# Gate and up products of a SwiGLU block: eight of eleven pairs by seven half-size products each, with weight sums made in memory

## The chip, the cores and the metric

The kernel runs on one core of a Trainium2 chip. The metric is the device time of one execution in microseconds, the median over runs. A core has TensorE (PE, with its weight loads as PEld), VectorE (DVE), ScalarE (ACT), GpSimd (POOL) and SyncE (SP, which here only issues DMAs). Each engine works through its own instructions in order and waits on semaphores for the others.

## What is computed

One encoder block over 512 tokens of width 1024, float32 in and out. Three gated branches are merged, and then comes the feed-forward part that the change touches:

```python
hf = _rms(x, g_ffn[l])
x = x + (jax.nn.silu(hf @ w_gate[l]) * (hf @ w_up[l])) @ w_down[l]     # D_FF = 2816
return _rms(x, g_final)
```

`w_gate` and `w_up` are 1024 x 2816, so each has 22 column tiles of 128, or 11 pairs of tiles.

## The kernel before

**Split products.** Every float32 operand is held as two fp32r tensors, a rounded high part and the rest, the low part. A product (`product`, L1652 to L1656) is three matmuls into one bank: high x high, low x high, high x low. So each weight tile of 128x1024 needs a load into `raw` (SP, `next_weights`), a rounding copy to `w_hi` (ACT, L619), and a subtraction `raw - w_hi` to `w_lo` (POOL, `low_weights`, L528). There are two slots of each (`NS`, `RAW` = 2). `w_rounded`, `w_ready` and `w_used` count the three steps and the tile's release by TensorE.

**Order of the stages.** The branches, then `w_out` (tiles `T_WO` to `T_FF`-1), then gate and up, then the down projection. Below, a "pair" is one of the 11 iterations of gate and up: four tiles (two gate, two up), each eight products of 128x512 in its bank, banks 0 to 3. TensorE's `feed` does them, in a loop from the second pair on.

**The normalisation.** The tokens' reciprocal root mean square isn't known when the first gate tile starts. `h_hi` and `h_lo` therefore hold x times the gain only, and VectorE multiplies each finished bank by `rstd` (`silu<-bank,rstd`, `parts<-bank,rstd`, `odd<-bank,rstd`).

**What follows a pair.** ACT applies SiLU to the gate half (L911); VectorE multiplies it with the up half, so that `parts[0:2]` and `odd` hold the hidden values of the pair: `a21, a11` and `a22, a12`, each a quarter of 128x256 (feature tile by token half). VectorE makes four sums of the quarters (`s_1` to `s_4`: L1037 twice, L1513, L1515). ACT's `split_hidden` rounds them into `ops` (128x1024, L916) and `op4` (128x256, L918), VectorE subtracts for their low parts (`ops<-parts,ops`, `op<-parts,op`), and `ff_lo` counts pairs done. SP stores `odd` to memory (`store_half`).

**The down projection** is already done by seven half-size products in place of eight. The sums of its weight blocks are made in memory: SP copies blocks of `w_down` to `mix_dram` (`copy_blocks`, two copies a pair, one behind each weight tile from tile `T_MIX` = 16 on), and POOL issues three accumulating DMAs a pair (`weight_sums`, one pair for every two weight tiles). Down weights are then loaded as units (`load_unit`, `round_unit`) and threes (`load_three`).

**Issue orders** are written out by hand for each engine; ACT's for a pair is: two SiLUs, three weight roundings, `split_hidden`, one weight rounding.

Of the kernel before, what the change touches and what calls it, by code (L numbers as in the profile page):

```python
# [16 lines left out]
P = 128  # L17
D = 1024
T = 512
M = 256  # L20
# [29 lines left out]
T_DN = T_FF + 4 * (KF // 2)  # L50
PAIRS = KF // 2
GROUPS = ((0, 2), (2, 5), (5, 8), (8, 11))
# [31 lines left out]
def build(nc, xt_d, xtok_d, mem_d, mtok_d, small_d, sgu_d, row_d, w_d, dn_d, mix_d, half_d, x1_d, out_d):  # L84
# [7 lines left out]
    with ExitStack() as ctx:  # L92
# [32 lines left out]
        h_lo = at("h_lo", o_h + 16384, [P, KD, T], R)  # L125

# [7 lines left out]
        x1_sq = [at(f"x1_sq{i}", o_a + ((6 + i) * PAIRS + 3) * 4 * HALF, [P, KD, KD, 32]) for i in range(2)]  # L134
# [9 lines left out]
        raw_d = at("raw_d", o_h + 12288, [P, TILE])  # L144
        raw_x = [at(f"raw_x{i}", o_x + 8192 + 4096 * i, [P, TILE]) for i in range(2)]
        raw_e = at("raw_e", o_e + 12288, [P, TILE])
        unit_raw = [raw[:, 0, :], raw[:, 1, :], raw_c[:, :], *(r[:, :] for r in raw_x), raw_d[:, :], raw_e[:, :]]
# [7 lines left out]
        unit_hi = [at("hi_x", o_x, [P, TILE], R)[:, :], w_hi[:, 0, :], w_hi[:, 1, :],  # L155
                   at("hi_c", o_h + 24576, [P, TILE], R)[:, :]]
        unit_lo = [at("lo_x", o_x + 4096, [P, TILE], R)[:, :], w_lo[:, 0, :], w_lo[:, 1, :],
# [43 lines left out]
        ops = at("ops", o_a, [P, 4, 2, PAIRS, HALF], R)  # L201
        op4 = at("op4", o_f, [P, 2, PAIRS, HALF], R)
        second = at("second", o_a + 2 * PAIRS * HALF * 4, [P, PAIRS, T])
        second_lo = at("second_lo", o_a + 2 * PAIRS * HALF * 4, [P, PAIRS, T], R)
        second_hi = at("second_hi", o_a, [P, PAIRS, T], R)
# [28 lines left out]
        rstd = at("rstd", o_d2 + 512, [P, T])  # L234
        o_d3 = o_d2 + 2560
# [21 lines left out]
        def sems(names):  # L257
            return [sem(n) for n in names.split()]

        raw_loaded = [sem(f"raw_loaded{i}") for i in range(RAW)]  # L260
# [10 lines left out]
        consts, wst_masked, hbias_ready, tables_ready = sems("consts wst_masked hbias_ready tables_ready")  # L271
# [5 lines left out]
        tok_sq, tok_std, diag_x, diag_m, wide_x, wide_m, rstd_ready, mrstd_ready = sems(  # L277
            "tok_sq tok_std diag_x diag_m wide_x wide_m rstd_ready mrstd_ready")
# [3 lines left out]
        var_ready, vstd_ready, vln_ready = sems("var_ready vstd_ready vln_ready")  # L282
# [8 lines left out]
        uc_ready, pow_ready, pads_ready, ca0_ready, ba_ready, ca_ready = sems(  # L291
            "uc_ready pow_ready pads_ready ca0_ready ba_ready ca_ready")
# [6 lines left out]
        mix_copied, mix_b12, mix_t2, mix_t4, half_stored = sems("mix_copied mix_b12 mix_t2 mix_t4 half_stored")  # L299
        unit_loaded = [sem(f"unit_loaded{i}") for i in range(7)]  # L300
        unit_half, unit_dve, p5_done, s1_ready, s5_ready = sems("unit_half unit_dve p5_done s1_ready s5_ready")
# [6 lines left out]
        row_loaded, out_dve, out_act, out_stored = sems("row_loaded out_dve out_act out_stored")  # L308
# [55 lines left out]

        block = ctx.enter_context(nc.Block())
# [3 lines left out]
        def _(sp):  # L369
# [11 lines left out]
            def next_weights(t):  # L381
                sp.wait_ge(w_ready, t + 1 - RAW)
                load_weights(t % RAW, t, w_d[t, :, :])
# [19 lines left out]
            def copy_blocks(i, j):  # L403

                if i:
                    sp.wait_ge(mix_copied, 32 * i)
                sp.dma_start(long_rows(mix_d[i, 2 * j:2 * j + 2]), long_rows(dn_d[2 * i + j]),
                             max_dma_last_dim=8 * TILE).then_inc(mix_copied, 16)

            for t in range(8, T_WO):  # L410
                next_weights(t)
                if 0 <= t - T_MIX < 2 * PAIRS:
                    copy_blocks(*divmod(t - T_MIX, 2))
                if t == T_J2 - 2:
                    sp.wait_ge(ba_ready, ROUNDS)
                    sp.wait_ge(ca_ready, ROUNDS)
                    for i in range(len(X_PARTS)):
                        load_x(i)
# [11 lines left out]
            def unit_split(eng, k):  # L430

                if k in UNIT_DVE:
                    eng.wait_ge(unit_dve, UNIT_DVE.index(k) + 1)
                else:
                    eng.wait_ge(w_ready, T_DN + UNIT_POOL.index(k) + 1)

            def load_unit(k):

                if k < 2:
                    sp.wait_ge(w_ready, T_DN - 1 + k)  # L440
                elif k == 5:
                    sp.wait_ge(w_used, T_DN)
# [5 lines left out]

            for t in range(T_WO, T_DN):
                next_weights(t)  # L450
                i, j = divmod(t - T_FF, 4)
# [4 lines left out]
                if i == 8 and j == 0:  # L456
                    sp.wait_ge(x1_moved, 16 * 8)
                    sp.wait_ge(mix_t4, 16 * PAIRS)
                    for k in (2, 3, 4):
                        load_unit(k)  # L460
# [19 lines left out]
            def load_half(g):  # L480
                k0, k1 = GROUPS[g]
                sp.dma_start(second[:, k0:k1, :], half_d[k0:k1, :, :].rearrange("k p n -> p k n")
                             ).then_inc(half_loaded[g], 16)

            for k in range(2):
                load_unit(k)
            load_unit(5)
# [3 lines left out]
            unit_split(sp, 4)  # L491
# [5 lines left out]
            sp.wait_ge(w_used, T_DN + 10)  # L497
# [8 lines left out]
            sp.wait_ge(w_used, T_DN + PAIRS)  # L506
            sp.dma_start(g_row[:, :], row_d).then_inc(row_loaded, 16)
# [13 lines left out]
        def _(pool):  # L521
# [25 lines left out]
            def two_rows(blocks):  # L547
# [1692 lines left out]
```

## Time and profile before

| | us |
|---|---|
| median of 3 runs | 772.1 (768.29 to 773.09) |
| profiled execution | 769.09 |
| its span, first to last instruction | 767.3 |
| outside the span | 1.8 |
| TensorE busy | 758.7 |
| VectorE busy | 490.0 |
| ScalarE busy | 354.9 |
| GpSimd busy | 343.2 |
| gate and up, from the first matmul to the last | 416.0 to 656.3 |

The span minus busy time is an engine's idle time. Matmuls are pipelined: a matmul's own duration in the profile (389 ns at 512 columns) is longer than the step from one to the next, so steps are what adds up. Gate and up take 240 of the 767 us.

### The profile page before, as it was taken

Reading aid. Unit: us, or ns where it says so; the run is one execution under the profiler, and the core shown is the slowest. Engines: PE = TensorE matmul, PEld = TensorE weight load, DVE = VectorE, ACT = ScalarE, POOL = GpSimd, SP = SyncE. Lnnn points to the kernel's source line nnn. Section 1 sums busy time; section 2 is a strip of 40 time slices with the busy share of each in tenths; the row PEclk is TensorE's granted clock in tenths of the full one; section 3 lists DMA queues with packets and bytes.
Section 4 is the critical chain, followed back from the end, with each engine's and each line's share of the span. In section 5 each row is a group of like instructions: output and inputs, shape, how many; then the busy total and the mean of one; then the engine's idle time right before and its main releaser. Section 6 shows DMA issues by size and latency. Waiting matters only on the chain.

```text
span 767.3 us, 9696 instructions
## 1 busy us (share of the span) xinstructions
PE 758.7 (99%) x3562; PEld 629.5 (82%) x3562; DVE 490.0 (64%) x708; ACT 354.9 (46%) x529; POOL 343.2 (45%) x202
## 2 busy tenths in 40 slices
PE   8999999999999999999999999999999999999997
PEld 7788887788888888888888888888888888888885
DVE  6999998684848484246767645455444455636686
ACT  6896567644545333634343423232323323435554
POOL 4456666356565543444444444444545455730000
PEclk9999999999999999999999999999999999999999
DMA  8743668199876752222233633333325333677853
GB/s 263 299 158 132 225 200 265 61 262 270 229 208 147 179 189 106 83 92 100 83 111 102 199 98 120 107 111 117 102 98 189 122 97 123 221 243 262 287 201 117
DMA packets 41491, 126.17 MB, mean 164 GB/s; under 512 B 4720, under 2 KB 6896, under 8 KB 38256
## 3 DMA queue, kind: packets, MB, share of 16 engines
q1 hardware_dynamic: 39376, 113.92, 42.9%
q0 software_dynamic: 1936, 11.54, 8.0%
q8 instruction: 21, 0.34, 0.2%
q10 hardware_dynamic: 144, 0.26, 0.1%
q14 instruction: 14, 0.11, 0.0%
HBM read 118.62 MB, written 30.15 MB: 194 GB/s over the span
## 4 chain that ended last, share of the span: by engine, by line
PE 91%; ACT 3%; DVE 3%; issue 1%; DMA 1%; SPq 0%; POOL 0%; ACTq 0%
PE bank L1654 24%; PE bank L1655 24%; PE bank L1656 24%; PE bank L2018 4%; PE bank L2019 4%; PE bank L2020 4%; ACT uc L679 1%; DVE s5p L1037 1%; PE bank L1895 1%; PE bank L1770 1%; PE bank L1787 1%; DMA xT<-xt_dram 1%; ACT w_hi L619 1%; DVE h_lo L1042 1%; PE bank L1869 0%
## 5 line engine op out<-in xcount | busy, mean ns | idle before, releaser
L528 POOL TENSOR_TENSOR w_lo<-raw,w_hi 128x1024 fp32r<-128x1024 f32 x90 | 221.5, 2461 | 273.8 <-ACT w_hi L619 273.8
L619 ACT ACTIVATE w_hi<-raw 128x1024 fp32r<-128x1024 f32 x112 | 118.7, 1060 | 311.4 <-PE bank L1656 306.8
L1654 PE MATMUL bank<-h_hi,w_hi 128*128 128x512 f32 x608 | 238.5, 392 | 0.2 <-POOL w_lo L533 0.2
L1656 PE MATMUL bank<-h_hi,w_lo 128*128 128x512 f32 x608 | 236.7, 389 | 0.0
L1655 PE MATMUL bank<-h_lo,w_hi 128*128 128x512 f32 x608 | 236.6, 389 | 0.0
L1654 PEld LDWEIGHTS bank<-h_hi,w_hi 128*128 128x128 f32 x608 | 114.2, 188 | 24.6 <-issue 1.0
L1655 PEld LDWEIGHTS bank<-h_lo,w_hi 128*128 128x128 f32 x608 | 114.2, 188 | 23.8 <-issue 0.5
L1656 PEld LDWEIGHTS bank<-h_hi,w_lo 128*128 128x128 f32 x608 | 114.1, 188 | 23.6
L533 POOL TENSOR_TENSOR w_lo<-raw,w_hi 128x512 fp32r<-128x512 f32 x48 | 67.1, 1417 | 50.3 <-ACT w_hi L619 43.2
L1037 DVE TENSOR_TENSOR lo<-raw,hi 128x1536 fp32r<-128x1536 f32 (+1 forms) x19 | 33.3, 1758 | 24.3 <-ACT hi L948 24.2
L1037 DVE TENSOR_TENSOR ops<-parts,ops 128x1024 f32 x11 | 25.9, 2352 | 27.8 <-ACT ops L916 24.6
L948 ACT ACTIVATE hi<-raw 128x1536 fp32r<-128x1536 f32 (+1 forms) x19 | 27.3, 1442 | 32.0 <-PE bank L2020 27.2
L1037 DVE TENSOR_TENSOR parts<-bank,rstd 128x512 f32<-128x512 f32 x11 | 7.6, 691 | 46.0 <-PE bank L1656 46.0
L1037 DVE TENSOR_TENSOR odd<-bank,rstd 128x512 f32<-128x512 f32 x11 | 7.6, 692 | 41.7 <-PE bank L1656 41.7
L1037 DVE TENSOR_TENSOR th<-bank,rstd 128x512 f32<-128x512 f32 x16 | 10.9, 682 | 30.7 <-PE bank L1656 30.6
L813 ACT ACTIVATE yaf<-bank 32x128 f32<-32x128 f32 x64 | 25.0, 390 | 4.5 <-PE bank L1870 3.8
L1037 DVE TENSOR_TENSOR parts<-odd,parts 128x256 f32<-128x256 f32 x11 | 26.4, 2398 | 0.4
L1654 PE MATMUL bank<-mg_hi,w_hi 128*128 128x512 f32 x64 | 25.0, 390 | 0.0
L1655 PE MATMUL bank<-mg_lo,w_hi 128*128 128x512 f32 x64 | 24.9, 389 | 0.0
L1656 PE MATMUL bank<-mg_hi,w_lo 128*128 128x512 f32 x64 | 24.9, 389 | 0.0
L1477 DVE SCALAR_TENSOR_TENSOR h_lo<-xT,small,h_hi 128x512 fp32r<-128x512 f32 x8 | 18.1, 2265 | 9.0 <-ACT h_hi L632 9.0
L679 ACT ACTIVATE uc<-uT 32x512 f32<-32x512 f32 x16 | 17.9, 1119 | 0.4
(331 smaller groups left out, 1411.4 us busy)
## 6 DMA issues: line engine op xcount, KB each, us to landing
raw<-w_dram SPq DMA_DIRECT2D x112, 512.0 KB, 3.3
mix_dram<-down_dram SPq DMA_DIRECT2D x22, 512.0 KB, 6.2
raw<-down_dram SPq DMA_DIRECT2D x26, 256.0 KB, 4.0
raw<-mix_dram SPq DMA_DIRECT2D x26, 256.0 KB, 3.7
mix_dram<-down_dram POOLq DMA_DIRECT2D x11, 512.0 KB, 9.6
mix_dram<-mix_dram POOLq DMA_DIRECT2D x22, 256.0 KB, 6.0
half_dram<-odd SPq DMA_DIRECT2D x11, 256.0 KB, 4.2
second<-half_dram SPq DMA_DIRECT2D x3, 768.0 KB, 6.5
```

Of the source, the lines that this page charges most:

```text
L528: nc.gpsimd.tensor_tensor(w_lo[:, s, :], raw[:, s, :], fv(w_hi[:, s, :]), ALU.subtract).then_inc(w_ready, 1)
L533: return nc.gpsimd.tensor_tensor(w_lo[:, s, c], raw[:, s, c], fv(w_hi[:, s, c]), ALU.subtract)
L619: nc.scalar.activation(w_hi[:, slot, :], raw[:, slot, :], ACT.Copy).then_inc(w_rounded, 1)
L679: nc.scalar.activation(dst[:, :, q, :], src[:, :, :, j], ACT.Copy).then_inc(uc_ready, 1)
L948: nc.scalar.activation(hi3[u % 2][:, 0:pieces(u), :], raw3[u % 3][:, 0:pieces(u), :], ACT.Copy).then_inc(rounded3, 1)
L1037: return V.tensor_tensor(out, a, b, op)
L1654: mm(out, a[0], b[0], start=first, stop=False)
L1655: mm(out, a[0], b[1], start=False, stop=False)
L1656: return mm(out, a[1], b[0], start=False, stop=last)
L2018: mm(bank[b][:, :], a[0], w[0], start=first, stop=False)
L2019: mm(bank[b][:, :], a[0], w[1], start=False, stop=False)
L2020: return mm(bank[b][:, :], a[1], w[0], start=False, stop=last)
```

## The change

The first three pairs (`PLAIN`) stay as they are. Each of the other eight (`TURNS`) becomes a turn: the 256 gate columns x 1024 rows are taken as a 2x2 grid of blocks (128 output features x 512 rows each), the normed tokens as a 2x2 grid (512 rows x 256 tokens), and the 2x2x2 block product is done by seven block products (`form_product`: 4 products of three 128x256 matmuls) instead of eight; the same for up. A turn has seven weight tiles (`FORMS`) of two blocks each, and 14 block products. What this takes:

- *Weight sums in memory:* 16 more jobs of copies and accumulating adds like those of the down projection, before these; the copies sit behind weight tiles 16 to 69 and the adds run to tile 78.
- *Operands:* the sums of token blocks (`t1` to `t4`) need tokens that are normed. VectorE multiplies x by gain and `rstd` (`norm_rows`), ACT rounds (`round_normed`), VectorE subtracts (`low_rows`), makes the sums (`forms_of_h`) and their low parts, all of it between the steps of the second and third pair. The plain pairs read copies in `hu_hi`, `hu_lo`.
- *Results:* the sums of products are made by VectorE from banks (15 `combine` a turn, 128x256); two products are first copied out of their banks by ACT (`copy_first`).
- *Weights:* a ring of three slots. Tiles 0, 2, 4, 6 of a turn get their low part from GpSimd, tiles 1, 3, 5 from VectorE (`low_weights`). Each tile is two DMAs of 256 KB.
- The loops of all engines are written out; semaphores are merged; `ops` is laid out by pair.

The core of the diff. Which engine finishes a tile, and GpSimd's share:

```diff
+        def low_done(eng, n):
+            i, j = divmod(n, FORMS)
+            if j % 2:
+                eng.wait_ge(w_ready_dve, 3 * i + j // 2 + 1)
+            else:
+                eng.wait_ge(w_ready, T_ST + 4 * i + j // 2 + 1)
...
+            for n in range(ST_TILES):
+                if n % FORMS % 2 == 0:
+                    pool.wait_ge(w_rounded, T_ST + n - 1)
+                    nc.gpsimd.tensor_tensor(ring_lo[n % 3], ring_raw[n % 3], fv(ring_hi[n % 3]), ALU.subtract
+                                            ).then_inc(w_ready, 1)
```

ScalarE, its new steps and its order in a turn:

```diff
+            def round_forms(n):
+                if n < 2:
+                    act.wait_ge(w_used, T_ST - 1 + n)
+                elif n > 2:
+                    act.wait_ge(product_done, 2 * (n - 2))
+                act.wait_ge(raw_loaded[n % 3], (0 if n % 3 == 2 else 16 * (T_ST // 2 - 1)) + 32 * (n // 3 + 1))
+                nc.scalar.activation(ring_hi[n % 3], ring_raw[n % 3], ACT.Copy).then_inc(w_rounded, 1)
+            def copy_first(turn, which):
+                act.wait_ge(product_done, 14 * turn + (1, 3)[which])
+                if which:
+                    act.wait_ge(ff_lo, PLAIN + turn + 1)
+                elif turn:
+                    act.wait_ge(combined, 15 * turn - 12)
+                out = (a_st[:, :], parts[:, 0, :])[which]
+                nc.scalar.activation(out, bank[4 - 4 * which][:, 0:HALF], ACT.Copy).then_inc(s_copied, 1)
...
+            for turn in range(TURNS):
+                n = FORMS * turn
+                round_forms(n + 2)
+                copy_first(turn, 0)
+                split_hidden(PLAIN + turn - 1)
+                round_forms(n + 3)
+                copy_first(turn, 1)
+                round_forms(n + 4)
+                round_forms(n + 5)
+                silu_forms(turn, 0)
+                round_forms(n + 6)
+                if turn + 1 < TURNS:
+                    round_forms(n + 7)
+                    round_forms(n + 8)
+                    silu_forms(turn, 1)
```

VectorE, in the second and third pair, and then in a turn:

```diff
+            scaled_gate(1, 0)
+            norm_rows(range(0, 4))
+            scaled_gate(1, 1)
+            norm_rows(range(4, 8))
+            scaled_up(1, 0)
+            low_rows(range(0, 5))
+            scaled_up(1, 1)
+            low_rows(range(5, 8))
+            hidden_sums(1)
+            low_hidden(1)
+            scaled_gate(2, 0)
+            forms_of_h()
+            scaled_gate(2, 1)
+            low_forms_a()
+            scaled_up(2, 0)
+            low_forms_b()
+            scaled_up(2, 1)
+            low_weights(1)
...
+            for turn in range(TURNS):
+                n, i = FORMS * turn, PLAIN + turn
+                hidden_sums(i - 1)
+                dve.wait_ge(s_copied, 2 * turn + 1)
+                combine(turn, 2, u2_st[0][:, :], gb, a_st[:, :], ALU.subtract)
+                low_weights(n + 3)
+                low_hidden(i - 1)
+                dve.wait_ge(s_copied, 2 * turn + 2)
+                combine(turn, 4, u2_st[1][:, :], ub, a21, ALU.subtract)
+                combine(turn, 5, g11, a_st[:, :], ga, ALU.add)
+                combine(turn, 6, g21, u2_st[0][:, :], gc, ALU.add)
+                low_weights(n + 5)
+                combine(turn, 7, u2_st[0][:, :], u2_st[0][:, :], gd, ALU.subtract)
+                dve.wait_ge(combined, 15 * turn + 5)
+                combine(turn, 7, g22, u2_st[0][:, :], gc, ALU.add)
...
+                if turn + 1 < TURNS:
+                    low_weights(n + 8)
+                dve.wait_ge(ff_silu, 2 * i + 1)
+                combine(turn, 12, a21, a21, g11, ALU.mult)
+                combine(turn, 13, a22, a22, uc_, ALU.add)
+                combine(turn, 14, a11, ud, u2_st[1][:, :], ALU.subtract)
+                dve.wait_ge(ff_silu, 2 * i + 2)
+                dve.wait_ge(combined, 15 * turn + 14)
+                tt(odd[:, :], odd[:, :], silu[:, 1, :], ALU.mult).then_inc(ff_act, 1)
+                dve.wait_ge(combined, 15 * turn + 15)
+                tt(a11, a11, g12, ALU.mult).then_inc(ff_act, 1)
```

TensorE in a turn:

```diff
+            for turn in range(TURNS):
+                n = FORMS * turn
+                low_done(pe, n)
+                if turn:
+                    pe.wait_ge(combined, 15 * turn - 5)
+                form_product(n, 0, 4, b11)
+                if turn == 0:
+                    pe.wait_ge(normed, KD + KD + 6)
+                form_product(n, 1, 5, t2)
+                low_done(pe, n + 1)
+                form_product(n + 1, 0, 0, b11)
+                form_product(n + 1, 1, 1, t2)
+                low_done(pe, n + 2)
+                pe.wait_ge(s_copied, 2 * turn + 1)
+                form_product(n + 2, 0, 4, b21)
+                if turn == 0:
+                    pe.wait_ge(normed, KD + KD + 8)
+                    pe.wait_ge(ff_u, 2 * PLAIN + 1)
+                else:
+                    pe.wait_ge(combined, 15 * turn)
+                form_product(n + 2, 1, 6, t3)
+                low_done(pe, n + 3)
+                form_product(n + 3, 0, 7, t1)
+                pe.wait_ge(s_copied, 2 * turn + 2)
+                form_product(n + 3, 1, 0, b21)
+                low_done(pe, n + 4)
+                form_product(n + 4, 0, 2, t3)
+                form_product(n + 4, 1, 3, t1)
+                low_done(pe, n + 5)
+                pe.wait_ge(combined, 15 * turn + 6)
+                form_product(n + 5, 0, 6, t4)
+                form_product(n + 5, 1, 7, b22)
+                low_done(pe, n + 6)
+                pe.wait_ge(combined, 15 * turn + 10)
+                form_product(n + 6, 0, 2, t4)
+                form_product(n + 6, 1, 3, b22)
```

In `combine(turn, count, ...)` VectorE first waits until `count` products of the turn are done.

## Rows read from the trace of the kernel before

**Rows 1.** Page, part 1: busy time, share of the span, instructions.
```profile
PE 758.7 (99%) x3562; PEld 629.5 (82%) x3562; DVE 490.0 (64%) x708; ACT 354.9 (46%) x529; POOL 343.2 (45%) x202
```

**Rows 2.** Waits of TensorE, whole span: who waited for whom, us, times, longest.
```profile
PE bank L1706 <- ACT h_hi L632: 1.5, 1, 1.5
...
PE bank L1654 <- POOL w_lo L533: 0.4, 2, 0.2
```

**Rows 3.** Windows, one pair: length, each engine's busy time, clock, DMA share, GB/s.
```profile
460.75:482.50 21.75, 21.75 (x98) 18.01 (x97) 10.41 (x12) 6.53 (x9) 10.04 (x4) 1.00 0.34 110
```

**Rows 4.** Timeline of TensorE, 83 to 87 us (start, duration): 512 columns, then 256.
```profile
83.86 0.39 PE L1656 MATMUL bank<-h_hi,w_lo 128*128 128x512 f32 x1
84.09 0.28 PE L1654 MATMUL bank<-m_hi,w_hi 128*128 128x256 f32 x1
...
86.84 0.28 PE L1656 MATMUL bank<-m_hi,w_lo 128*128 128x256 f32 x1
86.96 0.38 PE L1770 MATMUL bank<-kT,qT 128*128 128x256 f32 x1
```

**Rows 5.** Timeline of VectorE behind one pair.
```profile
505.01 0.69 DVE L1037 TENSOR_TENSOR odd<-odd,silu 128x512 f32<-128x512 f32 x1
505.74 2.50 DVE L1037 TENSOR_TENSOR parts<-odd,parts 128x256 f32<-128x256 f32 x1
...
508.94 0.42 DVE L1515 SCALAR_TENSOR_TENSOR parts<-odd,parts 128x256 f32<-128x256 f32 x1
511.82 2.43 DVE L1037 TENSOR_TENSOR ops<-parts,ops 128x1024 f32 x1 [2.45 <-ACT ops L916]
```

**Rows 6.** Timeline of GpSimd and ScalarE in the same stretch.
```profile
505.32 2.63 POOL L528 TENSOR_TENSOR w_lo<-raw,w_hi 128x1024 fp32r<-128x1024 f32 x1 [2.82 <-ACT w_hi L619]
510.76 2.40 POOL L528 TENSOR_TENSOR w_lo<-raw,w_hi 128x1024 fp32r<-128x1024 f32 x1 [2.81 <-ACT w_hi L619]
...
509.63 1.06 ACT L619 ACTIVATE w_hi<-raw 128x1024 fp32r<-128x1024 f32 x1 [4.38 <-PE bank L1656]
510.59 1.04 ACT L916 ACTIVATE ops<-parts 128x1024 f32 x1
511.54 0.40 ACT L918 ACTIVATE op<-parts 128x256 f32 x1
```

**Rows 7.** Timeline of GpSimd and VectorE in the first pair.
```profile
434.67 2.41 POOL L528 TENSOR_TENSOR w_lo<-raw,w_hi 128x1024 fp32r<-128x1024 f32 x1 [3.95 <-ACT w_hi L619]
...
435.16 0.68 DVE L1037 TENSOR_TENSOR parts<-bank,rstd 128x512 f32<-128x512 f32 x1
436.57 1.05 DVE L1037 TENSOR_TENSOR parts<-parts,silu 128x512 f32<-128x512 f32 x1 [0.72 <-ACT silu L911]
```

**Rows 8.** Groups by form, VectorE, 684 us to the end, where GpSimd is idle.
```profile
L1596 DVE SCALAR_TENSOR_TENSOR y_out<-y_out,orec,g_row 128x512 f32<-128x512 f32 x5 | 3.7, 749 | 0.1
...
L1037 DVE TENSOR_TENSOR lo<-raw,hi 128x1024 fp32r<-128x1024 f32 x2 | 2.4, 1222 | 0.2 <-ACT hi L948 0.2
...
L1037 DVE TENSOR_TENSOR y_out<-bank,y_out 128x256 f32<-128x256 f32 x2 | 0.8, 424 | 1.0 <-PE bank L1656 1.0
```

**Rows 9.** Timeline, GpSimd's halves back to back and VectorE's sums, last pair.
```profile
660.57 2.90 POOL L609 TENSOR_TENSOR lo_c<-raw_x,hi_c 128x512 fp32r<-128x512 f32 x2
...
659.38 1.50 DVE L1037 TENSOR_TENSOR parts<-parts 128x256 f32<-128x256 f32 x1
```

**Rows 10.** Page, part 6: DMA issues, KB each, median us to landing.
```profile
raw<-down_dram SPq DMA_DIRECT2D x26, 256.0 KB, 4.0
...
mix_dram<-down_dram POOLq DMA_DIRECT2D x11, 512.0 KB, 9.6
```

**Rows 11.** Timeline of GpSimd: adds issued behind a weight tile.
```profile
175.28 1.60 POOL L545 DMA_DIRECT2D mix_dram<-mix_dram  x2
176.32 1.43 POOL L545 DMA_DIRECT2D mix_dram<-down_dram  x1
```

**Rows 12.** Windows as in Rows 3, a stretch with weight sums in the background.
```profile
150.00:200.00 50.00, 50.00 (x284) 42.12 (x283) 32.05 (x60) 22.80 (x44) 28.80 (x21) 1.00 0.90 252
```

More of the change, by code:

```diff
@@ L925, in _ @@
             round_weights(T_FF + 7)
[L926 to L932 removed]
+            feed_forward(1)
+            round_normed(range(0, 4))
+            round_weights(T_FF + 8)
+            round_normed(range(4, 8))
+            round_weights(T_FF + 9)
@@ new lines, in norm_rows, with low_rows @@
+            def norm_rows(ks):
+                for k in ks:
+                    V.scalar_tensor_tensor(xT[:, k, :], xT[:, k, :], small[:, C_GFFN + k:C_GFFN + k + 1], rstd[:, :],
+                                           ALU.mult, ALU.mult).then_inc(normed, 1)
+            def low_rows(ks):
+                for k in ks:
+                    n = HALF if k < 4 else T
+                    dve.wait_ge(normed_hi, k + 1)
+                    tt(h_lo[:, k, 0:n], xT[:, k, 0:n], fv(h_hi[:, k, 0:n]), ALU.subtract).then_inc(normed, 1)
@@ new lines, in low_weights, with combine @@
+            def low_weights(n):
+                dve.wait_ge(w_rounded, T_ST + n - 1)
+                tt(ring_lo[n % 3], ring_raw[n % 3], fv(ring_hi[n % 3]), ALU.subtract).then_inc(w_ready_dve, 1)
+            def combine(turn, count, out, a, b, op):
+                dve.wait_ge(product_done, 14 * turn + count)
+                tt(out, a, b, op).then_inc(combined, 1)
+            for n in range(2):
+                scaled_gate(0, n)
+            for n in range(2):
+                scaled_up(0, n)
@@ L1523, in low_three @@
+            hidden_sums(PAIRS - 1)
+            low_hidden(PAIRS - 1)
             def low_three(u):
@@ L2004, in _ @@
                     pe.wait_ge(norms["f"]["lo"], k + 1)
-                    ins = product(bank[n][:, :], weight(n, k, 0, P, P), h(k), k == 0, k == KD - 1)
+                    ins = product(bank[n][:, :], weight(n, k, 0, P, P), hu(k), k == 0, k == KD - 1)
                 ins.then_inc(w_used, 1)
-            square_sum(norms["f"], 4, T, KD + 1)
+                if n == 0:
+                    square_sum(norms["f"], 4, T, KD + 1)
             feed(0, 1, ff_u)
             pe.wait_ge(norms["f"]["std"], 1)
-            with nc.tensor.Fori(1, KF // 2) as i:
+            for i in range(1, PLAIN):
@@ new lines, in _, with form_product @@
+            t4 = [(t4_hi[:, k, :], xT_r[:, 4 + k, 0:HALF]) for k in range(4)]
+            def form_product(n, half, b, x):
+                for k in range(4):
+                    c = slice(half * WB + k * P, half * WB + (k + 1) * P)
+                    ins = product(bank[b][:, 0:HALF],
+                                  (ring_hi[n % 3][:, c], ring_lo[n % 3][:, c]), x[k], k == 0, k == 3)
+                ins.then_inc(product_done, 1)
+            pe.wait_ge(normed, KD + KD)
+            pe.wait_ge(ff_g, 2 * PLAIN + 1)
@@ L2175, in _stream @@
         columns(w_out, c)
-    for f in range(0, KF, 2):
-        for w in (w_gate, w_up):
-            for n in range(2):
-                columns(w, f + n)
-    assert len(tiles) == T_DN
-    return np.stack(tiles)
+    assert len(tiles) == T_FF
+    pairs = [w[:, c * 2 * P:(c + 1) * 2 * P].reshape(2, 4, P, 2, P).transpose(3, 0, 2, 1, 4).reshape(4, P, WB)
+             for c in range(PAIRS) for w in (w_gate, w_up)]
+    return np.stack(tiles), np.stack(pairs)
 def kernel(**inputs):
```

420 lines of the change are left out of this document (279 added, 141 removed).

## The prediction

> **What bounds the kernel now.** I read the page's busy times first: TensorE is busy 758.7 of 767.3 us, the next engine, VectorE, 490 [rows 1]. The waits of TensorE come to a few microseconds in the whole span [rows 2]. So before the change every wait of the others is cover, and time can only be saved by issuing fewer matmul columns. Then the windows, cut at one pair: TensorE fills all 21.75 us, VectorE is busy 10.4, ScalarE 6.5, GpSimd 10.0, at the full clock [rows 3]. Last the timelines inside a pair, for how VectorE and GpSimd stand to each other, because the change takes TensorE's work down and puts VectorE's up.
>
> **What TensorE saves.** The first 256-column matmul of a tile starts at 84.09, the last at 86.84 and the next kind at 86.96: 24 matmuls in 2.87 us, 0.1196 each; a 512-column one steps 0.227 (96 of them in 21.75) [rows 3, 4]. A turn has 14 x 12 = 168 of the short ones: 20.1 us, and a block product is 1.435. Seven eighths of 21.75 would be 19.0, so half of the gain is lost to the shorter form. What is left is 1.66 us a turn, 13.3 for eight turns, if TensorE never waits: 769.1 - 13.3 = 755.8.
> By the Trainium skill ("TensorE: Matmul & The Clock Gate", Back-to-back issue gap) a 256-column matmul takes 262 cycles at 2.4 GHz, 109 ns, so a turn would be 18.3 us and the forecast below some 6 us lower. The rows show 120 ns, and they decide.
>
> **GpSimd and VectorE exclude each other.** GpSimd's subtraction takes 2.40 when alone. At 505.32 it is issued while VectorE works until 505.70, and takes 2.63, to 507.95; VectorE's next operation, a 256-element sum of two SBUF tensors, starts at 505.74 and takes 2.50, to 508.24 [rows 5, 6]. At 511.82 VectorE's 1024-element subtraction takes 2.43: GpSimd ends at 513.16, and 1.09 remain [rows 5, 6]; with GpSimd idle it takes 1.22 [rows 8]. So one waits for the other's whole instruction. A VectorE operation with an operand from a bank is not touched: 0.68 us in the middle of a GpSimd subtraction, while the next one, of two SBUF tensors, ends 0.55 behind GpSimd's end [rows 7].
>
> **A turn, step by step.** Durations: VectorE 1024 elements 1.22, 512 0.69, 256 0.42 [rows 5, 8]; ScalarE's rounding 1.06, and 0.96 from one start to the next, the split 1.35 in all, a 256 copy 0.40 [rows 6]; GpSimd 2.40. A product is done 0.16 after its last issue slot (0.28 less 0.12) [rows 4]. Zero is the start of the turn's first product; tiles are 0 to 6.
> ScalarE may round tile 2 only when all 14 products of the last turn are done: 0.2 to 1.3, and then GpSimd wants its subtraction. VectorE does the last combine to 0.8 and the 512-element product with SiLU to 1.5; GpSimd, waiting, gets in between as at 505.7, and holds VectorE to 3.9. Then one product and four sums, 5 x 0.42: the sums of the hidden values are done at h = 6.0.
> From there on it is one chain, since ScalarE and VectorE each have these steps one behind the other: `split_hidden` to h+1.4; rounding of tile 3, h+2.4; VectorE's low part of tile 3, h+3.6; `low_hidden`, 1.22 and 0.41, h+5.2; `copy_first(turn, 1)`, which waits for it, h+5.7; rounding of tile 4, queued behind that copy, h+6.7; GpSimd's low part, h+9.2; and only then products 9 to 14, 6 x 1.435 = 8.6. The turn ends at h + 17.8 = 23.8.
> TensorE wants tile 3 at 8.6 and gets it at 9.6, wants the copy (its bank) at 10.0 and gets it at 11.7, wants tile 4 at 13.2 and gets it at 15.2: stalls of 1.0, 0.7 and 2.0. None is long, so I leave the clock at 1.00.
> The rest fits behind: tile 5's low part is VectorE's, waits for GpSimd to 15.2, done 16.4, and two combines to 17.2, before product 11 at 18.1. Tile 6: GpSimd 16.4 to 18.8, needed at 21.0. Next tile 0: its slot's load goes out at 15.3, lands 4.0 later and 0.4 for the second half's issue [rows 10], so 19.7, rounded 20.7, GpSimd to 23.1, needed at 23.8. One more microsecond of landing would cost 0.2 a turn.
> So a turn takes 23.8 against a pair's 21.75: +2.1. Ends of this price: -1.66 if nothing waits, and +3.6 if GpSimd takes tile 6 at 15.2 ahead of VectorE's tile 5 (then product 11 starts 1.5 later). I take VectorE first: where GpSimd's halves run back to back VectorE's small sums get in after each, 1.50 and the like [rows 9].
>
> **The second and third pair.** Zero is the start of the second pair; TensorE would reach tile 1 of the first turn at 2 x 21.75 + 2.9 = 46.4. VectorE has, in order, up to that tile's low part: five up steps of two operations (6.7), four gate steps (2.8), two sets of sums and low parts (6.4), eight `norm_rows` at 0.75 (6.0) [rows 8], eight `low_rows` (4.4), `forms_of_h` 4 x 1.22, its low parts 4 x 1.22, and 1.2: 37.3 us. GpSimd has nine subtractions in the stretch, 21.6, and nearly all of VectorE's work is of two SBUF tensors. Together 58.9; stepping through the two queues, with the waits for ScalarE, gives 59.9: tile 1 is late by 13.5. On the way `scaled_gate(2, 1)` comes behind `forms_of_h` at 45.3, ScalarE's SiLU waits for it and the rounding of tile 0 stands behind the SiLU, so that the first product starts at 49.6 and not 43.5: the two pairs lose 2, for weight tiles whose rounding stands behind the new steps, and 4 are a wait before it. Then h is 59.9 + 1.6 = 61.5, and the first turn ends at 79.3, where three pairs took 65.2: +14.1. Bounds: 0 if VectorE's 37.3 hid in 46.4, and 18 if each of four more waits costs a microsecond.
>
> **Other parts, costed at nothing or little.** The 16 added jobs of sums in memory run under tiles 16 to 78. Where 11 such jobs run now, DMA engines are busy 0.90 of the time and TensorE 50.0 of 50 us [rows 12]; the three issues of a job occupy GpSimd 2.5 us, from 175.28 to 177.75 [rows 11], in its idle time, once per two tiles (10.9 us), and the slowest add lands in 9.6 [rows 10], before the next job asks. If they came late, GpSimd's wait would hold the next tile's low part; with 10.9 against 9.6 I give it 0, at most 2 us. The 15 combines are in the turn above. Behind the last turn the down units are no longer loaded ahead: unit 3 is loaded only after the last product, lands at +4.6, is rounded at 6.1 and its first half done at 7.5, needed at 8.2; units 4 and 5 are closer. 0.5 us.
>
> **Sum.** 769.1 + 14.1 + 7 x 2.1 + 0.5 = 798.4 us. The profiled execution lies 3 below the median of before, 772.1; I give 798.
>
> **The rivals.**
> *TensorE stays the bound, 756.* It needs h below 2.3 and the pairs' extra work hidden. For it: VectorE's work in a turn, uncontended, is 3 x 1.22 + 1.63 + 4 x 0.42 for weights, hidden parts and sums, 15 x 0.42 for combines and 1.1 for the products: 14.4 of 20. Against: the order is a chain, and h alone holds GpSimd's 2.4. Chance 7%. This is the other side: it decides if TensorE finds tile 4 ready at 13.2.
> *No exclusion.* If two-SBUF operations ran beside GpSimd, h were 3.6 and a turn 21.4, the pairs' work hidden: 769.1 - 8 x 0.35 = 766. The trace speaks against it twice (2.43 and 2.50). 3%. The Trainium skill says that GpSimd and VectorE's 2p instructions block each other ("Advanced Engine Details and Errata", VectorE Performance Modes) and that a two-tensor operation cannot enter that mode ("VectorE: DVE Perf Modes", Mode 2×_2P); by the two alone this would be the case, 766, and the trace disagrees: 2.43 us against 1.22.
> *The pairs hide, the turns don't.* 769.1 + 8 x 2.1 = 786. For it: slack of 9 us by busy time. 12%.
> *VectorE wins the race at 1.3*, so that its product and sums come before GpSimd's tile 2: turns 21.5, the pairs as above: 781. 4%.
> *GpSimd takes tile 6 first*: turns 25.4, 8 x 1.5 more: 811. The requests lie 0.1 us apart. 15%.
> *Ring loads late*: 3.5 MB a turn where a pair moved 2, at 0.34 of the DMA time now [rows 3]; if a load took 3 us longer each turn would lose some 2.5 more: 818. 7%.
> The forecast itself: 52%.
>
> **The range.** 780 to 814 takes in the forecast, the three rivals at 781, 786 and 811: 83% less what falls beside. A measurement of this kernel can tell about 1% from no change. Faster by more than that is the first rival, 0.07; within it the second and the low edge of the others, 0.08; slower 0.85.
>
> **What would show it.** In the trace after: turns of 23.8 in the windows; TensorE waiting for GpSimd's low part of tile 4 (the longest of its waits, 2 us, eight times), for ScalarE's bank copy, and for VectorE's tile 3; a wait of 4 before the first product of the first turn and one of 6.5 before its third; VectorE's second SiLU product or first sum at 2.4 and more beside GpSimd. A matmul step other than 0.12, or turns with no wait before product 9, would make it wrong.

## The result, and the profile after

The changed kernel takes 798.45 us (794.74 to 801.24, 4 runs) against 770.69 for the kernel before (4 runs, one more than ahead of the prediction): a ratio of 1.036 (1.030 to 1.042). The forecast was 798. The total is right; of its terms two were too large and one was missing, and they cancel. The profiled execution took 801.24 us, the slowest of the four; its span is 799.5 us, 32.2 more than before, and all that is read from the trace below belongs to it and not to the median.

The page of the changed kernel, parts 1, 2 and 6 (slices are 20 us each here):

```profile
PE 760.9 (95%) x4138; PEld 652.7 (82%) x4138; DVE 566.2 (71%) x844; ACT 391.4 (49%) x581; POOL 384.5 (48%) x250
...
PE   9999999999999999999999898799988888999997
...
DMA  8743687389888998999988753355655555777853
...
raw<-w_dram SPq DMA_DIRECT2D x68, 512.0 KB, 5.0
...
raw<-ff_dram SPq DMA_DIRECT2D x33, 256.0 KB, 2.9
```

TensorE is busy as long as before [rows 1], but idle time has come in: seven eighths of the products didn't give back what the short matmuls and the waits took. The DMA engines are at least 0.8 busy in every slice from 160 to 440 us.

The waits of TensorE (us in total, times, longest):

```profile
PE bank L1946 <- POOL w_lo L698: 15.1, 8, 3.2
PE bank L1946 <- DVE w_lo L1204: 6.9, 3, 4.8
PE bank L1946 <- POOL w_lo L612: 5.3, 5, 3.5
PE bank L1946 <- ACT parts L1042: 1.8, 7, 0.3
```

These are, in order: GpSimd's low part of a turn's tile, once in each turn (3.2 before the first turn's first product, then 1.7 at tile 4 of each of the others; before: 0.4 in all, [rows 2]); VectorE's backlog before the first turn's third product (4.8) and its low part of tile 3 in two later turns (1.1 and 1.0); mostly a plain pair's weight tile that came late (3.5); the copy out of the bank.

Windows, cut near the steps (as [rows 3] of before):

```profile
441.90:457.10 15.20, 11.69 (x52) 9.37 (x51) 6.56 (x7) 4.32 (x5) 6.39 (x5) 0.98 0.82 228
457.10:463.40 6.30, 6.28 (x15) 4.95 (x16) 6.20 (x6) 0.63 (x1) 3.81 (x3) 0.51 0.79 203
463.00:492.80 29.80, 29.80 (x132) 24.38 (x130) 27.33 (x32) 10.81 (x18) 11.05 (x5) 1.00 0.39 120
492.80:520.00 27.20, 18.86 (x123) 18.30 (x123) 20.20 (x26) 12.88 (x17) 9.43 (x4) 0.81 0.36 115
567.00:590.00 23.00, 20.94 (x170) 20.33 (x170) 16.55 (x27) 10.18 (x14) 10.63 (x5) 1.00 0.55 174
```

One turn is the 23 us of the last line, with 2 us without a matmul; the second line is 6.3 us at half clock, which nothing in the forecast stood for. Nor did it have anything for the fourth line, the first turn, whose clock is 0.81: its matmuls behind the waits of 3.2 and 4.8 us ran in part at half clock. Behind the second of them:

```profile
505.90:511.20 5.30, 5.28 (x25) 5.28 (x26) 3.22 (x7) 2.31 (x3) 0.00 (x0) 0.51 0.71 232
```

That is 24 matmuls in 5.2 us, where at 0.1196 they would take 2.9: 2.3 us. The same steps by their first and last instruction, one line of the tile views for each:

```profile
L1946 PE MATMUL bank<-hu_hi,w_hi x96: 389/389/792, 419.1 to 492.1; 128*128 128x512 f32 x96
...
L1204 DVE TENSOR_TENSOR silu<-a_st,bank x8: 409/410/410, 513.3 to 676.4; 128x256 f32<-128x256 f32 x8
```

The second is one combine, once a turn: (676.4 - 513.3) / 7 = 23.30 us a turn. The down projection starts at 688.1 (656.3 before). So the 32.2 us are:

| step | forecast | measured |
|---|---|---|
| before feed-forward (starts at 419.1, before 416.0) | 0 | +3.1 |
| three plain pairs, 73.6 against 66.3 | +2.0 | +7.3 |
| first turn, 32.3 against 21.75 | +12.1 | +10.5 |
| seven turns, 23.30 against 21.75 | +14.7 | +10.9 |
| down projection and end, 111.4 against 111.0 | +0.5 | +0.4 |
| sum | +29.3 | +32.2 |

(The first turn is what is left between 492.7, the last plain matmul's step, and 688.1 less seven turns. Cut at the first product of the second turn, 525.6, it is 32.8 and the seven turns are 162.5, 23.2 each. The column adds up to the profiled execution; the median lies 2.8 us lower.)

The turn's chain, as the forecast walks it. GpSimd, then VectorE, from the end of the second turn's products, about 548.5, on (start, duration):

```profile
549.86 2.40 POOL L698 TENSOR_TENSOR w_lo<-raw,w_hi 128x1024 fp32r<-128x1024 f32 x1 [3.24 <-ACT w_hi L1032]
561.30 2.37 POOL L698 TENSOR_TENSOR w_lo<-raw,w_hi 128x1024 fp32r<-128x1024 f32 x1 [9.04 <-ACT w_hi L1032]
...
549.90 2.91 DVE L1204 TENSOR_TENSOR odd<-odd,silu 128x512 f32<-128x512 f32 x1
...
554.30 0.42 DVE L1688 SCALAR_TENSOR_TENSOR parts<-odd,parts 128x256 f32<-128x256 f32 x1
...
557.11 1.23 DVE L1204 TENSOR_TENSOR w_lo<-raw_c,w_hi 128x1024 fp32r<-128x1024 f32 x1 [2.04 <-ACT w_hi L1032]
558.25 1.22 DVE L1204 TENSOR_TENSOR ops<-parts,ops 128x1024 fp32r<-128x1024 f32 x1
...
560.31 0.42 DVE L1204 TENSOR_TENSOR u_st<-bank,parts 128x256 f32<-128x256 f32 x1 [0.51 <-ACT parts L1042]
```

VectorE's 512-element product takes 2.91 and not 0.69, since GpSimd has just begun tile 2; the hidden sums end at 554.7, h = 6.2 (forecast 6.0); tile 3's low part, then the hidden low parts, then ScalarE's copy (the 0.51 in front of 560.31), then GpSimd's tile 4, which ends at 563.67: 9.0 behind the sums, forecast 9.2. At the first turn's end VectorE was a little ahead (product at 526.10 to 526.78, GpSimd at 526.88), the first sum waited instead, and h was 5.3.

The turn shown isn't the usual one. The seven spacings of the combine are 23.46, 23.93, 22.97, 22.97, 23.84, 22.97 and 22.98 us. In the two long ones GpSimd gets in right in front of VectorE's 512-element product (the turn shown) or right behind it, and tile 3 comes about a microsecond late; in the others VectorE gets both its products through first, only the first sum waits, and TensorE has at most 0.1 us to wait at tile 3. What goes with it is a load. ScalarE's rounding of the next turn's tile 1, in a short turn and in the turn shown, then VectorE's low part of the same tile:

```profile
522.87 1.06 ACT L1032 ACTIVATE w_hi<-raw_c 128x1024 fp32r<-128x1024 f32 x1 [1.82 <-PE bank L1948]
546.66 1.06 ACT L1032 ACTIVATE w_hi<-raw 128x1024 fp32r<-128x1024 f32 x1 [2.54 <-DMA raw<-sum_dram]
...
523.96 1.23 DVE L1204 TENSOR_TENSOR w_lo<-raw_c,w_hi 128x1024 fp32r<-128x1024 f32 x1 [0.67 <-ACT w_hi L1032]
547.75 1.23 DVE L1204 TENSOR_TENSOR w_lo<-raw,w_hi 128x1024 fp32r<-128x1024 f32 x1 [1.49 <-ACT w_hi L1032]
```

In both long turns the rounding waits for the load and not for TensorE, VectorE is some 0.8 us later with all that follows, and GpSimd gets in an operation or two sooner.

### The profile page after: what moved, and what is told of

The parts are those of the page before. It is cut to its first block, busy times and chain, and to the rows that moved or that the text cites. A ratio compares the mean times of both kernels' runs of the same rounds, so it can differ in the third digit from the quotient of the medians.

```text
span 799.5 us, 10980 instructions
## 1 busy us (share of the span) xinstructions
PE 760.9 (95%) x4138; PEld 652.7 (82%) x4138; DVE 566.2 (71%) x844; ACT 391.4 (49%) x581; POOL 384.5 (48%) x250
## 4 chain that ended last, share of the span: by engine, by line
PE 52%; DVE 13%; DMA 11%; POOL 9%; issue 8%; ACT 6%; SPq 0%; DVEq 0%; ACTq 0%; POOLq 0%
PE bank L1946 12%; PE bank L1948 12%; PE bank L1947 12%; DMA raw<-w_dram 7%; POOL w_lo L612 4%; DVE parts L1204 4%; PE bank L2368 3%; PE bank L2369 3%; PE bank L2370 3%; ACT w_hi L1032 3%; DMA raw<-ff_dram 3%; DVE odd L1204 2%; DVE ops L1204 2%; POOL w_lo L698 1%; ACT w_hi L718 1%
## 5 line engine op out<-in xcount | busy, mean ns | idle before, releaser
L1946 PE MATMUL bank<-h_hi,w_hi 128*128 128x512 f32 (+1 forms) x512 | 175.9, 344 | 12.9 <-DVE w_lo L1204 6.9
L1948 PE MATMUL bank<-h_hi,w_lo 128*128 128x512 f32 (+1 forms) x512 | 172.7, 337 | 0.0
L1947 PE MATMUL bank<-h_lo,w_hi 128*128 128x512 f32 (+1 forms) x512 | 172.7, 337 | 0.0
L1947 PE MATMUL bank<-xT_r,w_hi 128*128 128x256 f32 x192 | 55.3, 288 | 0.0
L1946 PE MATMUL bank<-hu_hi,w_hi 128*128 128x512 f32 x96 | 39.3, 410 | 4.4 <-POOL w_lo L612 4.0
L1947 PE MATMUL bank<-hu_lo,w_hi 128*128 128x512 f32 x96 | 38.6, 402 | 0.0
L1948 PE MATMUL bank<-hu_hi,w_lo 128*128 128x512 f32 x96 | 38.4, 400 | 0.0
L1947 PEld LDWEIGHTS bank<-xT_r,w_hi 128*128 128x128 f32 x192 | 37.9, 197 | 0.0
L1946 PE MATMUL bank<-t_hi,w_hi 128*128 128x256 f32 x128 | 37.4, 293 | 0.3 <-DVEq L1730 0.3
L1948 PE MATMUL bank<-t_hi,w_lo 128*128 128x256 f32 x128 | 37.1, 290 | 0.0
```

Of the source, the lines that this page charges most:

```text
L1946: mm(out, a[0], b[0], start=first, stop=False)
L1947: mm(out, a[0], b[1], start=False, stop=False)
L1948: return mm(out, a[1], b[0], start=False, stop=last)
```

## Experiments

The kernel before ran beside each group of kernels: 769.1 us beside the first four, 769.3 beside the next four, 769.1 beside the last two. "FF" below is the start of feed-forward, "turn" the mean spacing of the same combine in the profiled execution (the first spacing still holds the end of the first turn and is often the odd one). Where an expectation names no kernel it is the changed one, 798.45.

| kernel | us (median) | ratio to before | FF | turn |
|---|---|---|---|---|
| changed | 798.45 | 1.036 | 419.1 | 23.30 |
| e1 no jobs for gate and up | 791.69 | 1.030 | 414.5 | 23.14 |
| e2 low parts on VectorE | 777.02 | 1.012 | 415.2 | 20.31 |
| e3 own buffer for the copy | 785.74 | 1.021 | 417.5 | 21.90 |
| e4 rounding ahead of the copy | 804.18 | 1.045 | 416.8 | 24.21 |
| e5 before, with the jobs | 774.42 | 1.006 (1.004 to 1.008) | 418.8 | |
| e6 jobs eight tiles earlier | 798.43 | 1.038 | 425.5 | 23.31 |
| e7 e2 + e3 + e6 | 777.26 | 1.011 | 423.0 | 20.27 |
| e8 e7 + four plain pairs | 770.49 | 1.0005 (0.9988 to 1.0021) | 424.3 | 20.13 |
| e9 e2 + e3 + four plain pairs | 765.83 | 0.996 (0.9945 to 0.9977) | 416.4 | 20.38 |
| e10 four plain pairs alone | 785.80 | 1.021 | 416.9 | 23.32 |

### What makes a turn 23 us: e2, e3, e4

**e2: all seven low parts on VectorE.**

```diff
-            for n in range(ST_TILES):
-                if n % FORMS % 2 == 0:
-                    pool.wait_ge(w_rounded, T_ST + n - 1)
-                    nc.gpsimd.tensor_tensor(ring_lo[n % 3], ring_raw[n % 3], fv(ring_hi[n % 3]), ALU.subtract
...
                 hidden_sums(i - 1)
+                low_weights(n + 2)
                 dve.wait_ge(s_copied, 2 * turn + 1)
```

(and `low_weights` of tiles 4, 6 and of the next turn's first tile at their places).

> All seven low parts of a turn on VectorE, GpSimd idle in the turns. Theory (a turn is one chain, and GpSimd's 2.4 us stands in it twice, once as a lock on VectorE's sums and once as tile 4's low part): a turn falls from 23.2 to about 20.8, and the first turn starts some 2 earlier, 777 us. Rival (VectorE is short of time): 4 x 1.22 more on top of 16.6 busy us a turn leaves the turn at 24 or more, 800 to 806.

Measured 777.02 us, a turn of 20.31, as a rule 20.16: TensorE's bound of 20.1 is all but reached. VectorE has more to do and the kernel is 21 us faster, so it was never short of time. Groups by form, VectorE, 525 to 640 us; first the changed kernel, then this one (count | busy us, mean ns):

```profile
L1204 DVE TENSOR_TENSOR w_lo<-raw,w_hi 128x1024 fp32r<-128x1024 f32 x10 | 17.5, 1754 | 13.0 <-ACT w_hi L1032 13.0
L1204 DVE TENSOR_TENSOR parts<-odd,parts 128x256 f32<-128x256 f32 x5 | 8.4, 1673 | 0.2
```

```profile
L1195 DVE TENSOR_TENSOR w_lo<-raw,w_hi 128x1024 fp32r<-128x1024 f32 x27 | 32.8, 1220 | 4.6 <-ACT w_hi L1023 4.6
...
L1195 DVE TENSOR_TENSOR parts<-odd,parts 128x256 f32<-128x256 f32 x5 | 2.1, 425 | 0.2
```

The same operations take 1.22 and 0.43 once GpSimd is still. The edit takes away two things at once, the lock and the 2.40 us of GpSimd's own low part of tile 4 (VectorE makes it in 1.22); how the 3.0 us of a turn divide between them no run tells.

**e3: the second copy in a buffer of its own.**

```diff
-                if which:
-                    act.wait_ge(ff_lo, PLAIN + turn + 1)
+                if which and turn:
+                    act.wait_ge(combined, 15 * turn - 8)
...
-                out = (a_st[:, :], parts[:, 0, :])[which]
+                out = (a_st[:, :], b_st[:, :])[which]
```

(`b_st` lies in the place of `rstd` and small constants that are done; VectorE waits for its own hidden low parts before it writes `silu`.)

> ScalarE's second copy of a product goes to a buffer of its own, so that it no longer waits for VectorE's low parts of the hidden sums, and the rounding of tile 4 behind it comes some 3 us earlier. Theory (the chain through that copy): GpSimd gets tile 4 done at h+6.0 instead of h+9.2, then VectorE's tile 5 and two combines bound product 11; a turn of 21.9, 1.3 less, 788 us. Rival (the copy costs only what TensorE waits for it by name, 0.3 us a turn): 796.

Measured 785.74, a mean turn of 21.90, the figure that the chain gave. It is made up of one spacing of 24.70 and six of 21.4 to 21.5, so the chain as I walked it is 0.5 too long. The wait that the profile names for the copy was 1.8 us in the whole kernel (7 times, 0.3 at most); taking the copy out of the chain brought 12.7, 9.8 of it in the seven spacings. The price of a link isn't the wait under its own name, but what is queued behind it: here the rounding of tile 4.

**e4: the rounding of tile 4 ahead of the copy.**

```diff
-                copy_first(turn, 1)
                 round_forms(n + 4)
+                copy_first(turn, 1)
```

> One exchange in ScalarE's order: tile 4 is rounded ahead of the second copy instead of behind it. Theory (GpSimd and VectorE exclude each other): GpSimd's tile 4 then starts in front of VectorE's low parts of the hidden sums and holds them 2.4 us, so the copy and product 8 come later by about that; turn the same or up to 0.4 longer, 798 to 801. Rival (the order on ScalarE is all that is wrong, the two engines work side by side): tile 4 is ready 3 us earlier, its wait of 1.9 goes in each turn, 785.

Measured 804.18, a mean turn of 24.21: 0.9 longer, twice what I had allowed for, and the opposite of what the rival gives. GpSimd (first line) starts tile 4 at 556.47 while VectorE works; VectorE's next operation waits for all of it:

```profile
556.47 2.47 POOL L698 TENSOR_TENSOR w_lo<-raw,w_hi 128x1024 fp32r<-128x1024 f32 x1 [4.79 <-ACT w_hi L1032]
...
555.48 1.23 DVE L1204 TENSOR_TENSOR w_lo<-raw_c,w_hi 128x1024 fp32r<-128x1024 f32 x1 [2.05 <-ACT w_hi L1032]
556.62 3.40 DVE L1204 TENSOR_TENSOR ops<-parts,ops 128x1024 fp32r<-128x1024 f32 x1
```

3.40 against 1.22 in the changed kernel. TensorE's wait moves to the copy (waits of TensorE):

```profile
PE bank L1946 <- ACT parts L1042: 17.1, 7, 2.4
```

The mean doesn't show what the exclusion costs, though. The spacings are 25.86, 24.71, 23.21, 24.68, 23.20, 24.64 and 23.20. The short ones are 0.2 longer than the changed kernel's short ones, as expected. In the long ones of 24.7 the matmuls behind the wait of 2.4 us run at half clock. Windows from that wait on, in the second and the third turn:

```profile
536.10:539.70 3.60, 3.52 (x17) 3.53 (x17) 3.32 (x7) 1.88 (x4) 0.00 (x0) 0.53 0.35 109
560.80:564.40 3.60, 3.51 (x29) 3.51 (x30) 3.50 (x8) 2.35 (x4) 0.64 (x1) 1.00 0.32 107
```

That costs some 1.5 us, behind four of the seven waits. An estimate from these rows: 4 x 1.5 = 6, about the 5.7 us that e4 is slower than the changed kernel. The expectation had no term for it.

So the order on ScalarE alone mends nothing as long as the two engines exclude each other. Together e2, e3 and e4 leave no room for VectorE's sum of work as the bound of a turn, nor for the ring's loads, but for the 0.9 us in two turns of seven.

### What the background jobs cost: e1, e5, e6

The late tile of the second plain pair, in the changed kernel. Timeline of ScalarE and SyncE, then the tile view of `raw`, 436 to 460 us:

```profile
453.49 1.06 ACT L718 ACTIVATE w_hi<-raw 128x1024 fp32r<-128x1024 f32 x1 [8.48 <-DMA raw<-ff_dram]
...
440.94 7.03 SPq L426 DMA_DIRECT2D raw<-ff_dram  x2
...
DMA to landing us min/median/max: 3.6/7.1/12.5
```

A load of 512 KB landed 12.5 us after its issue; in the same stretch of before the slowest took 3.8. TensorE stood 3.5 us and then did its next 14 matmuls at 0.427 us each, at a granted clock of 0.51 in the window shown above, which is 1.2 GHz.

**e1: without the 16 jobs** (the turns load plain blocks where sums would be).

```diff
-FF_JOBS = 2 * TURNS
+FF_JOBS = 0
...
-                    blocks = src[job] if src is sum_d else src[2 * PLAIN + job]
+                    blocks = ff_d[2 * PLAIN + job]
```

> The changed kernel without the 16 jobs that sum gate and up weights in memory; the turns load plain blocks of the weights in place of the sums, so the sums are left out of what is computed. The trace of the changed kernel has feed-forward starting 3.1 us later than before, and in its second pair a weight tile that lands 12.5 us after its issue, a gap of 3.5 us and 14 matmuls at half clock (3 us more), while the DMA engines are 0.8 to 1.0 busy. Theory: all of that is the jobs' traffic and goes, but VectorE's work of the second and third pair then becomes what is waited for again (third product of the first turn at 60 us after the second pair's start instead of 64), so of 9.6 us some 7 to 9 come back: 789 to 792. Rival, that the late tile has another cause (the x1 stores, which both kernels have): 797 to 799.

Measured 791.69: 6.8 less. The three plain pairs take 67.0 us in place of 73.6, without a late tile, but TensorE's wait for VectorE before the first turn's third product grows from 4.8 to 5.3: part is taken back there, as expected.

**e5: the kernel before with 16 more jobs**, of down weights and of the same size, at the changed kernel's tiles. With them come two small parts of the change in how work is issued: the loads of x go out one behind each weight tile and not all at once, and GpSimd's issues are written out further.

```diff
-                if 0 <= t - T_MIX < 2 * PAIRS:
-                    copy_blocks(*divmod(t - T_MIX, 2))
+                next_copy(t)
```

> The kernel before, with 16 more jobs of sums in memory of the same size at the same tiles (of down weights, nobody reads the result). One part of the change alone. Theory (the jobs' traffic makes weight loads late once it fills the DMA engines): 3 us by the start of feed-forward, and up to 6.5 in its first pairs, where the x1 stores come on top: 774 to 780. Rival (the jobs are hidden, and the late tile needs the rest of the change): 770 to 772.

Measured 774.42, 1.0058 of before (1.0040 to 1.0076), and the same late tile, with little else of the change in the kernel. Feed-forward begins at 418.8 in the profiled execution, 2.8 later than before. Timeline of TensorE (the one long wait in its second pair):

```profile
455.05 0.79 PE L1690 MATMUL bank<-h_hi,w_hi 128*128 128x512 f32 x1 [2.48 <-POOL w_lo L551]
```

So about 5 us of the 28 are the memory traffic by itself. Whether the late tile needs the x1 stores beside the jobs was not tried: both kernels have the stores, and no run leaves them out.

**e6: the jobs eight weight tiles earlier.**

```diff
-T_MIX = T_VU
+T_MIX = T_QK
```

> The changed kernel with the jobs started eight weight tiles earlier (tile 8 in place of 16), so that they end eight tiles earlier, before feed-forward's second pair. Theory: the late tile of the second pair and its cold matmuls go, part of the 3.1 us before feed-forward too; VectorE's backlog keeps some: 790 to 794. Rival (the same traffic costs the same wherever it lies): 798.

Measured 798.43: nothing gained. The late tile is gone (plain pairs 67.0 us), but feed-forward starts at 425.5, 6.4 later (in a profiled execution of 803.52, 5 above the median; e7 and e8, with the same early jobs, have 423.0 and 424.3): the same loads now meet the first stages' own. Windows of this kernel, 50 to 150 us, where TensorE was busy 99.8 of 100 us before:

```profile
50.00:100.00 50.00, 48.82 (x260) 41.84 (x258) 41.08 (x68) 28.92 (x43) 31.91 (x27) 1.00 0.79 246
100.00:150.00 50.00, 45.39 (x211) 34.94 (x210) 44.39 (x61) 30.76 (x57) 30.75 (x30) 0.97 0.82 246
```

My expectation of 790 to 794 was wrong and the rival's number right: traffic isn't free earlier, it only meets other loads. That it costs the same wherever it lies doesn't follow: e8 and e9 below differ in nothing but the tile at which the jobs start, and their medians lie 4.7 us apart.

### What is lost before the first turn: e7, e8, e9, e10

**e7** puts e2, e3 and e6 together.

> All low parts of the turns on VectorE, the copy in its own buffer, and the jobs eight tiles earlier. Theory: turns at TensorE's bound, 20.3 to 20.8, no late tile; what stays is VectorE's backlog in the second and third pair, some 8 to 10 us: 767 to 772. Rival (VectorE is the bound of a turn): 780 or more.

Measured 777.26, 5 us above the expected range: the turns are at 20.27, but it carries e6's loss (feed-forward at 423.0), and TensorE still waits 7.5 us for VectorE around the first turn. It is no faster than e2.

**e10: four plain pairs in the changed kernel**, the norming and the sums spread over three pairs.

```diff
-PLAIN = 3
+PLAIN = 4
...
+            scaled_gate(2, 0)
+            low_rows(range(0, 5))
+            scaled_gate(2, 1)
+            low_rows(range(5, 8))
+            scaled_up(2, 0)
+            forms_of_h()
...
+            scaled_gate(3, 0)
+            low_forms_a()
+            scaled_gate(3, 1)
+            low_forms_b()
```

> The changed kernel with four plain pairs and nothing else changed: the norming of the tokens and their sums spread over three pairs. Theory (the first part of the loss is VectorE's backlog in two pairs): the waits before the first turn's first and third product go from 3.2 and 4.8 to under 2 in all, the late tile is gone with the two jobs fewer, one turn fewer loses 1.5: 798 less 5, 6 and 1.5 less the first turn's longer chain, 782 to 787. Rival (the backlog is not it, the first turn waits for the ring's loads): 790 or more.

Measured 785.80, 12.7 less than the changed kernel with one turn fewer. Its turns are as long as ever (23.32), and the long waits before the first turn are gone: no wait of TensorE in this kernel is over 1.7 us. The two before the first turn's first and third product are 1.5 and 1.7, 3.2 in all where I expected under 2. The edit also ends the jobs earlier, so the late tile's share of the 12.7 isn't told apart here.

```profile
PE bank L1959 <- POOL w_lo L698: 13.2, 8, 1.7
PE bank L1959 <- DVE w_lo L1210: 3.8, 3, 1.6
```

**e8 and e9** have four plain pairs, all low parts of the turns on VectorE, and the copy's own buffer. In e8 the jobs start at tile 8, in e9 at tile 16, as in the changed kernel.

> As the last, and with four plain pairs in place of three, so that the norming of the tokens and their sums spread over three pairs (seven turns are left, 14 jobs). Theory (what is left of the loss is VectorE's backlog in two pairs): it goes nearly whole, for one turn's gain of 1 us: 760 to 766, below both kernels. Rival (the loss before the first turn isn't VectorE's backlog): 768 to 772, as the last one.

> Four plain pairs, all low parts of the turns on VectorE, the copy in its own buffer, and the jobs at their old place (from tile 16). With 14 jobs they end four tiles earlier than in the changed kernel, ahead of the tile that was late. The version with the jobs from tile 8 lost some 8 us before feed-forward (it began at 424.3 us against 416.0 before). Theory (what the jobs cost depends on what other loads they meet, and between tile 16 and 73 they meet few): feed-forward begins at 415 to 419, no late tile, 761 to 765, below both kernels. Rival (the traffic costs the same wherever it lies): 769 to 772, with a late tile in the second pair again.

e8: 770.49, equal to before and above its expected range: the backlog is gone, the early jobs' loss stays (424.3). e9: 765.83, 0.996 of before (0.9945 to 0.9977), a little over the expected 761 to 765: feed-forward begins at 416.4 and there is no late tile, since 14 jobs end before it. It is the fastest version, by 0.4%. Its turns are 20.16 as a rule, so seven should save 7 x 1.59 = 11.1 us; the kernel is 3.3 faster (769.1 - 765.8). Cut at TensorE's steps, the profiled execution is 0.4 later at feed-forward, its four plain pairs take 89.4 in place of 88.0, the seven turns 144.8 in place of 152.2 (7.4 saved, since the first turn has a wait of 1.9 and 1.4 us of half clock behind it), and the down projection and end 113.3 in place of 111.0. Waits of TensorE in e9:

```profile
PE bank L1959 <- DVE w_lo L1204: 1.9, 1, 1.9
PE bank L1959 <- POOL w_lo L609: 1.5, 3, 0.5
```

## Why the prediction was right, and where it wasn't

**Matmul steps.** 0.1196 us for 256 columns held: e2's turns, at 20.16 as a rule, leave 0.1 beside 168 x 0.1196. It held at full clock only. The forecast left the clock at 1.00 everywhere, also behind its own waits of 4 and 6.5.

**The exclusion of GpSimd and VectorE** was read from two coincidences in the trace of before [rows 5, 6] and carried the forecast. e2 shows it by taking it away (1.22 and 0.43 again), e4 by one more of it (3.40 in place of 1.22, and the wait of 2.4 at the copy); e4's longer time is no measure of it, being mostly clock.

**The turn** was forecast at 23.8 and measured at 23.30: +2.1 against +1.55 over a pair, 4 us too much over seven turns. The order of the links was right, and TensorE waits at tile 4 as forecast, though 1.7 us and not 2.0. The part over was in the stalls before it: the forecast had 1.0 at tile 3, the trace has that in two turns only, and 0.3 at the copy in place of 0.7. VectorE was some tenths ahead of my walk at the turn's end. The walk lets GpSimd in behind the 512-element product. It holds nearly to the letter in the two turns of 23.9 and 23.8, where a late load holds VectorE up; in the others GpSimd gets in one operation later and the turn is 22.97. The rival at 21.5, with all the sums in front of GpSimd, is in none of them.

**The second and third pair and the first turn.** The mechanism stood (a wait of 3.2 before the first product, forecast 4, and of 4.8 before the third, forecast 6.5), and e10 and e1 tell it from the jobs. It was sized 1.6 too high in the first turn. The two waits together are 8.0 in place of 10.5; part of why may be that TensorE was itself late by then, so that VectorE caught up while the late tile held the pair (without the late tile, in e1, they are 3.9 and 5.3). That the total is off by less is luck: from the third product to the turn's end the forecast has 19.4 us with 2.2 of stalls in it, and the trace has 19.7 with no stall at all and 2.3 of half clock.

**The background jobs** were the step that failed. "I give it 0, at most 2 us": the term was 5 us or more (e5 +5, e1 -6.8). I had judged it by a stretch at 0.90 of the DMA engines' time without a TensorE wait [rows 12] and by the spacing of the adds on GpSimd [rows 10, 11]. Neither asks what a weight load takes to land behind jobs and x1 stores together. The rows of before had the stores, but never with the jobs on top.

**The tail** (+0.5 forecast, +0.4 measured) held.

So the forecast came near partly because 5.4 us too much in the turns and the first turn stood against 8.4 that were missing before them. That leaves it 2.9 below the profiled execution; that it meets the median to half a microsecond is because that execution lies 2.8 above the median.

What stays open: how the 3.1 us before feed-forward in the profiled execution divide. Other kernels with the same jobs there began feed-forward at 415.2 to 417.5, and e5 at 418.8, so part of it may belong to that execution; I didn't repeat its profile. Open too is how much of the plain pairs' +7.3 would stay without the x1 stores, and why e9's down projection takes 2.3 us more than before.

## What to carry to other kernels

Price a link of a chain by what is queued behind it on each engine and not by the wait that carries its name: a copy with 1.8 us of waits was worth 12.7, 9.8 of them in the turns. And price a wait of TensorE with the clock behind it: the same 2.4 us wait cost another 1.5 in four turns of seven. Where VectorE and GpSimd both work on pairs of SBUF tensors, add their times as if they were one engine, and try the work on one of them alone. A fast multiplication that saves an eighth of the columns saves far less when its matmuls are half as long (here 7.6%), and the additions, their operands and the extra weight traffic must fit into that.

## What the runs showed of the hardware that I had not expected

- Traffic between places in memory that keeps the DMA engines 0.8 to 1.0 busy can delay one 512 KB load to 12.5 us (3.2 to 3.8 in the same stretch of before), while the median over the kernel only rises from 3.3 to 5.0. A mean hides it.
- TensorE gaps of 2.5 us (e5), 3.5 and 4.8 us were followed by half clock: behind the one of 3.5, 14 matmuls at 0.427 us, 3 us more than at full clock, so the gap cost nearly twice itself. The waits of 1.7 us in the turns were not followed by it. In between the length of the gap doesn't tell: in e4 waits of 2.4 us were followed by some 15 matmuls at 0.213 us four times of seven, and a wait of 1.95 us stands in the first turn of both e9 and e8, with half clock behind it in e9 and none in e8. Windows from the wait's end, e9 first:

```profile
507.90:512.00 4.10, 4.08 (x21) 4.10 (x22) 4.03 (x8) 0.76 (x3) 0.00 (x0) 0.58 0.57 162
```

```profile
515.90:519.00 3.10, 3.10 (x26) 3.10 (x27) 3.06 (x6) 0.45 (x2) 0.00 (x0) 1.00 0.59 169
```
